# Head sums on rounded halves, and the second chunk's solve on the opposite half: a hybrid layer on one core

## The reference, cut to what matters

```python
kk = hs(k * k_k)
kk = kk / jnp.maximum(jnp.sqrt(jnp.sum(kk * kk, axis=-1, keepdims=True)), 1e-12)
...
def step(S, inp):
    r_t, w_t, k_t, v_t, kk_t, a_t = inp
    sa = jnp.einsum('bhij,bhj->bhi', S, -kk_t)
    S = (S * w_t[:, :, None, :] + sa[..., None] * (kk_t * a_t)[:, :, None, :]
         + v_t[..., None] * k_t[:, :, None, :])
    return S, jnp.einsum('bhij,bhj->bhi', S, r_t)
...
mean = jnp.mean(o, axis=-1, keepdims=True)
var = jnp.mean(jnp.square(o - mean), axis=-1, keepdims=True)
...
bonus = jnp.sum(rh * kh * r_k, axis=-1, keepdims=True) * vh
```

## Time and profile before

| | |
|---|---|
| median of 3 runs | 3245.78 us (3243.72 to 3246.97) |
| the profiled execution | 3246.72 us |
| its span, first to last instruction | 3244.7 us |
| TensorE busy | 3171.4 us (98%) |
| DVE busy | 1625.4 us (50%) |
| ACT busy | 1022.0 us (31%) |
| POOL busy | 232.5 us (7%) |
| mean granted clock of TensorE | 0.997 |

### The profile page before, as it was taken

How to read it: one execution, slowest core, us unless ns; L and a number is a source line. 1 busy time by engine, 2 the same in 40 slices (tenths; PEclk the granted TensorE clock), 3 DMA queues, 4 the chain that set the end, 5 groups by cost and what they waited for, 6 DMA issues and landing times.

```text
span 3244.7 us, 65733 instructions
## 1 busy us (share of the span) xinstructions
PE 3171.4 (98%) x27835; PEld 2663.8 (82%) x27835; DVE 1625.4 (50%) x2742; ACT 1022.0 (31%) x1858; POOL 232.5 (7%) x229
## 2 busy tenths in 40 slices
PE   8999999999999999999999999999999999999998
PEld 6777778877777878877777878998777789999997
DVE  6566554567766573454553256304555525432224
ACT  5444333344443443232222034302333312310001
POOL 0021100011011000111110000001111100000000
PEclk9999999999999999999999999999999999999999
DMA  4454443376666753554444673265343445465556
GB/s 160 155 190 161 147 154 97 104 233 203 196 215 215 254 188 97 163 157 144 138 143 146 193 237 102 92 210 167 125 124 125 134 158 168 147 192 181 176 176 196
DMA packets 269442, 532.27 MB, mean 164 GB/s; under 512 B 34016, under 2 KB 37728, under 8 KB 269152
## 3 DMA queue, kind: packets, MB, share of 16 engines
q1 hardware_dynamic: 269152, 528.07, 50.6%
HBM read 415.97 MB, written 112.08 MB: 163 GB/s over the span
## 4 chain that ended last, share of the span: by engine, by line
PE 89%; DVE 6%; DMA 2%; ACT 1%; issue 1%; SPq 0%; POOL 0%; DVEq 0%; ACTq 0%; POOLq 0%
PE PS L824 76%; PE PS L863 6%; PE PS L921 1%; PE PS L976 1%; DMA y<-xres 1%; DMA wl<-weight_lo 1%; DMA raw<-w 1%; DVE wl L1585 1%; PE PS L997 1%; PE PS L1147 1%; DVE op L2077 1%; PE PS L911 0%; PE PS L1161 0%; PE PS L1165 0%; ACT L1176 0%
## 5 line engine op out<-in xcount | busy, mean ns | idle before, releaser
L824 PE MATMUL PS<-hh,wh 128*128 128x512 f32 x1864 | 766.2, 411 | 0.9 <-ACT gst L1235 0.9
L824 PE MATMUL PS<-hh,wl 128*128 128x512 f32 x1864 | 728.9, 391 | 0.0
L824 PE MATMUL PS<-hl,wh 128*128 128x512 f32 x1864 | 727.9, 391 | 0.0
L1195 ACT ACTIVATE wh<-raw 128x512 fp32r<-128x512 f32 x452 | 284.1, 630 | 481.2 <-PE PS L824 365.7
L824 PEld LDWEIGHTS PS<-hh,wh 128*128 128x128 f32 x1864 | 350.3, 188 | 91.2 <-issue 14.3
L1585 DVE TENSOR_TENSOR wl<-raw,wh 128x512 fp32r<-128x512 f32 x452 | 321.6, 714 | 194.4 <-ACT wh L1195 189.2
L824 PEld LDWEIGHTS PS<-hh,wl 128*128 128x128 f32 x1864 | 350.4, 188 | 76.0
L824 PEld LDWEIGHTS PS<-hl,wh 128*128 128x128 f32 x1864 | 351.1, 188 | 73.7 <-issue 8.1
L824 PE MATMUL PS<-hh_last,wh 128*128 128x272 f32 x1280 | 266.1, 289 | 2.0 <-DVE xres L1717 2.0
L824 PE MATMUL PS<-hl_last,wh 128*128 128x272 f32 x1280 | 264.6, 288 | 0.0
L824 PE MATMUL PS<-hh_last,wl 128*128 128x272 f32 x1280 | 263.2, 287 | 0.0
(11 more groups left out here) (284 smaller groups left out, 4815.7 us busy)
## 6 DMA issues: line engine op xcount, KB each, us to landing
wh<-weight_hi SPq DMA_DIRECT2D x500, 256.0 KB, 2.7
wl<-weight_lo SPq DMA_DIRECT2D x500, 256.0 KB, 3.0
raw<-w SPq DMA_DIRECT2D x186, 512.0 KB, 3.6
weight_hi<-wh SPq DMA_DIRECT2D x164, 256.0 KB, 4.4
weight_lo<-wl SPq DMA_DIRECT2D x164, 256.0 KB, 4.7
raw<-w SPq DMA_DIRECT2D x76, 256.0 KB, 3.4
gate_scratch<-gst SPq DMA_DIRECT2D x48, 256.0 KB, 3.8
gb<-gate_scratch SPq DMA_DIRECT2D x24, 512.0 KB, 5.1
```

What stands on the lines that cost most here:

```text
L824: mm = pe.matmul(PS[:, bank(t) + f, 0:t.cols], wt[:, cols], mov[:, m, (t.half + f) * t.cols:(t.half + f + 1) * t.cols], start=(first and a ...
L1195: act.activation(wh[h % 4][:], src, ACT.Copy).then_inc(hi_done, 1)
```

## The change

The four head sums take two matmuls each, on a rounded part and a remainder of what is summed, against `head`, a copy of the ones matrix in fp32r that ACT makes once at the start. The rounded parts are written by ACT (`ksh`, `bh`, `mh`, `vh`), the remainders by DVE (`ksl`, `bl`, `ml`, `vl`), and the square `osq` moves from ACT to DVE as `sq`. The second chunk's solve goes from the half where it was to the opposite one: `home to own` becomes `own to home` and the reverse, S1 goes home to own and is interleaved over both chunks, and `pt1`, `yo` and `x` of the second chunk change halves on the way, which puts them on DVE in two half-tile operations each.

```diff
@@ steps @@
-        s += ["n1", "zp"] + ["lwm"] * sample + ["scan", ...]
+        s += ["ksl", "n1", "zp"] + ["lwm"] * sample + ["scan", ...]
...
-        s += ["at", "rt", "pc", "btE", "btO", "ktE", "ktO", "atl", "bv"]
-        s += each("lmE", "lmO", "ydE", "ydO") + each("xd", "svE", "svO")
+        s += ["at", "rt", "pc", "btE", "btO", "ktE", "ktO", "atl", "bl", "bv"]
+        s += each("lmE", "lmO", "ydE", "ydO") + ["pt1E1", "pt1O1"] * (not sample) + each("xd", "svE", "svO")
+        s += ["yoE1", "yoO1"] * (not sample)
@@ TensorE @@
+            def head_sum(bank_, n, hi, lo):
+                pe.matmul(PS[:, bank_, 0:n], head[:], hi[:].rearrange("p a w -> p (a w)")[:, 0:n], start=True, stop=False)
+                return pe.matmul(PS[:, bank_, 0:n], head[:], lo[:].rearrange("p a w -> p (a w)")[:, 0:n], start=False, stop=True)
...
                 yield pr.t("BO")
-                pe.wait_ge(G, pr.at("G", "bo2"))
+                pe.wait_ge(V, pr.at("V", "bl"))
                 step("bo")
-                pe.matmul(PS[:, 3, 0:4 * W], mat[:, M_HEAD], flat(cc), start=True, stop=True).then_inc(Tn, 1)
+                head_sum(3, 4 * W, pph, ccl).then_inc(Tn, 1)
...
                 yield pr.t("S1")
                 for c in pr.chs:
                     pe.wait_ge(V, pr.at("V", f"xd{c}"))
                     pe.wait_ge(A, pr.at("A", f"tok{c}"))
-                    for j in range(4):
-                        tiles(c, home, home, 5 + 2 * c, 0, of(yd[c]), of(xd[c]), j)
-                    for j in range(4):
-                        mm = tiles(c, home, home, 5 + 2 * c, 256, of(xd[c]), of(yd[c]), j)
+                for j in range(4):
+                    for c in pr.chs:
+                        tiles(c, home, own, 5 + 2 * c, 0, of(yd[c]), of(xd[c]), j)
+                for j in range(4):
+                    for c in pr.chs:
+                        mm = tiles(c, home, own, 5 + 2 * c, 256, of(xd[c]), of(yd[c]), j)
...
                 yield pr.t("MEAN")
-                pe.wait_ge(V2, pr.at("V2", f"oO{pr.chs[-1]}"))
+                pe.wait_ge(V2, pr.at("V2", "ml"))
...
                 yield pr.t("VAR")
-                pe.wait_ge(A2, pr.at("A2", "osq"))
+                pe.wait_ge(V2, pr.at("V2", "vl"))
@@ ScalarE @@
+                act.wait_ge(A, pr.at("A", "ksq"))
+                go("ksh", v4(cch), v4(pp), ACT.Copy)
...
+                yield pr.t("PTR", 0.8)
+                act.wait_ge(G, pr.at("G", "bo2"))
+                act.wait_ge(V, pr.at("V", "pc"))
+                go("bh", v4(pph), v4(cc), ACT.Copy)
...
+                yield pr.t(f"DO{pr.chs[-1]}", 0.6)
+                act.wait_ge(V2, pr.at("V2", f"oO{pr.chs[-1]}"))
+                go("mh", fl(oph), fl(oo), ACT.Copy)
                 yield pr.t("MEAN", 0.6)
                 act.wait_ge(V2, pr.at("V2", "oc"))
-                go("osq", fl(oo), fl(op), ACT.Square)
+                go("vh", fl(yol), fl(op), ACT.Square)
@@ VectorE @@
+                yield pr.t("ZA", 0.2)
+                dve.wait_ge(A, pr.at("A", "ksh"))
+                if pr.before:
+                    dve.wait_ge(G, pr.before.at("G", "lb"))
+                tt_("ksl", fl_(ktl), fl_(pp), fl_(cch), ALU.subtract)
...
+                yield pr.t("PV", 0.9)
+                dve.wait_ge(A, pr.at("A", "bh"))
+                tt_("bl", fl_(ccl), fl_(cc), fl_(pph), ALU.subtract)
                 yield pr.t("BO", 0.4)
                 dve.wait_ge(Tn, pr.at("T", "bo"))
...
+                    if c:
+                        own("ydO1")
+                        for par, name in enumerate(("E", "O")):
+                            r = home(1, par)
+                            tt_(f"pt1{name}1", pts[1][0][half_rows(par)], yd[1][r], mrep(M_XD, 4, r.start, r.stop, 64, 128), ALU.add)
...
-                    tt_(f"x{c}", yo[c][:], zl[c][:], q8(b1_), ALU.add)
+                    if c == 0:
+                        tt_("x0", yo[0][:], zl[0][:], q8(b1_), ALU.add)
+                    for par, name in enumerate(("xE1", "xO1")) if c else ():
+                        r = home(1, par)
+                        tt_(name, yo[1][r], zl[1][half_rows(par)], q8(b1_, r), ALU.add)
...
+                dve.wait_ge(A2, pr.at("A2", "mh"))
+                tt_("ml", fl_(yol), fl_(oo), fl_(oph), ALU.subtract)
                 yield pr.t("MEAN", 0.25)
...
+                own("oc")
+                tt_("sq", fl_(oo), fl_(op), fl_(op), ALU.mult)
+                dve.wait_ge(A2, pr.at("A2", "vh"))
+                own("sq")
+                tt_("vl", fl_(ool), fl_(oo), fl_(yol), ALU.subtract)
```

More of the change, by code:

```diff
@@ L249, in steps @@
     if engine == "V2":
-        s = ["x0", "saE0", "saO0"] + (["st10", "st20", "oE0", "oO0", "x1", "saE1", "saO1"] if not sample else [])
+        s = ["x0", "saE0", "saO0"] + (["st10", "st20", "oE0", "oO0", "xE1", "xO1", "saE1", "saO1"] if not sample else [])
         c = chs[-1]
-        return s + [f"oE{c}", f"oO{c}", f"st1{c}", f"st2{c}", "oc", "on", "lg", "ob", "gate"]
+        return s + [f"oE{c}", f"oO{c}", f"st1{c}", f"st2{c}", "ml", "oc", "sq", "vl", "on", "lg", "ob", "gate"]
     if engine == "A":
-        s = ["ksq", "vt", "z0", "z1", "z2", "z3", "a0", "a1", "a2", "a3", "ex", "es", "n2", "n3", "pm", "p", "ip"]
-        return s + by("ptr") + ["ath"] + by("tok", "xy2", "xy4", "x8", "d", "zl", "g", "h") + ["gc"]
+        s = ["ksq", "vt", "ksh", "z0", "z1", "z2", "z3", "a0", "a1", "a2", "a3", "ex", "es", "n2", "n3", "pm", "p", "ip"]
+        return s + by("ptr") + ["bh", "ath"] + by("tok", "xy2", "xy4", "x8", "d", "zl", "g", "h") + ["gc"]
     if engine == "A2":
-        return each("o1") + ["osq", "v1", "v2", "rwh"]
+        return each("o1") + ["mh", "vh", "v1", "v2", "rwh"]
     if engine == "G":
-        return ["kk", "cm", "kkn", "bo1", "bo2"] + by("pt1") + each("yoE", "yoO") + ["lb"]
+        return ["kk", "cm", "kkn", "bo1", "bo2", "pt10", "yoE0", "yoO0", "lb"]
     if engine == "G2":
@@ L441, in hybrid_layer @@
         hw0, ha0, hka = (new(n, [128, 4]) for n in ("hw0", "ha0", "hka"))
-        mat = new("mat", [128, M_MEAN, 128])
+        mat = new("mat", [128, M_HEAD, 128])
+        head = new("head", [128, 128], F32R)
         lora = new("lora", [128, 2, 512])
@@ L935, in front @@
                 yield pr.t("KG")
-                pe.wait_ge(V, pr.at("V", f"sub{pr.chs[-1]}"))
+                pe.wait_ge(V, pr.at("V", "ksl"))
+                if pr.first:
+                    pe.wait_ge(head_in, 1)
                 step("kn")
-                pe.matmul(PS[:, 4, 0:4 * W], mat[:, M_HEAD], flat(pp), start=True, stop=True).then_inc(Tn, 1)
+                head_sum(4, 4 * W, cch, ktl).then_inc(Tn, 1)
                 yield pr.t("PTR")
@@ L1047, in front @@
                     for c in pr.chs:
[L1048 removed]
+                        mm = tiles(c, own, home, 4 + 2 * c, 0, of(xd[c]), of(pts[c][2]), j)
                         if j == 3:
@@ L1130, in tail @@
                     for j in range(4):
-                        first = tiles(c, own, own, b1_, 0, lambda r, j, par: ra[r, j * n + c, 1, :], of(st), j)
-                        mm = tiles(c, own, other, b0_, 0, of(st), lambda r, j, par: ra[r, j * n + c, 0, :], j)
+                        first = tiles(c, own, home, b1_, 0, lambda r, j, par: ra[r, j * n + c, 1, :], of(st), j)
+                        mm = tiles(c, own, away, b0_, 0, of(st), lambda r, j, par: ra[r, j * n + c, 0, :], j)
                     step(f"q0{c}")
@@ L1547, in front @@
                 yield pr.t("XT", 0.05)
[L1548 to L1558, removed]
+                own("bo2")
+                pool.wait_ge(V, pr.at("V", "ydO0"))
+                tt_("pt10", pts[0][0][:], yd[0][:], mrep(M_XD, 4, c0=64, c1=128), ALU.add)
+                own("pt10")
+                for par, name in enumerate(("yoE0", "yoO0")):
+                    r = home(0, par)
+                    tt_(name, yo[0][r], lm[0][r, par, :, CH:128], mrep(M_YD, 4, r.start, r.stop, 64, 128), ALU.mult)
+                    own(name)
                 pool.wait_ge(V, pr.at("V", "bv"))
```

74 lines of the change are left out of this document (43 added, 31 removed).

## The result

The changed kernel takes **3309.9 us** (median of 4 runs, 3304.9 to 3312.5), the kernel before 3244.8 us beside it: ratio **1.0199**, 95% interval 1.0183 to 1.0215, 65 us slower. The forecast was 3284 us, range 3258 to 3304: right in direction, 26 us too low, and the time lies above the range. The profiled execution took 3307.4 us (span 3305.5), 60.7 us above that of before.

The account below looks back on a forecast made before the run. TensorE, busy 98% of the span, was taken as the bound. The terms summed to +38.8 us on the profiled 3246.7 us, giving 3285.5 us profiled and 3284 us as a median; range 3258 to 3304 us.

Parts of the forecast that it names:

- Sums: Head sums on TensorE: two rounded products take 0.46 us instead of 0.85 for one f32 sum; -25.6 us.
- S1: Solve stage S1 on four array quarters, interleaved over both chunks: 1.09 instead of 2.00 us a double pair; -14.6 us.
- Rival D: S1 doesn't gain because half its weight loads are exposed: +37 instead of -14.6 us, 3336 us; chance 0.04.
- BO: TensorE's sum at BO waits for `bl`, queued on DVE behind `atl`; +50 us over seventeen pairs.
- LM: TensorE's waits before LM go, since DVE catches up while TensorE stands; -2.9 us.
- VAR: The sum at VAR is released 0.75 us later by `sq`, `vh`, `vl`; only the first two pairs feel it; +1.4 us.
- MEAN: The sum at MEAN is released 1.65 us later, behind `ml`, partly hidden by spare time; +14 us.
- `x1` in halves: Two half-tile operations on DVE add 0.42 us ahead of `ds1`, where TensorE waited 7 times; +2.9 us.
- The clock: After 8 of the new stalls TensorE runs at 1.2 GHz for 3.42 us, costing 1.7 us each; +13.6 us.
- A: TensorE's clock holds, since the new stalls are single and products follow each; 3271 us; chance 0.22.
- B: DVE is no longer behind at BO, so its 50 us and the clock's 13.6 fall away; 3222 us; chance 0.09.
- C: More waits than counted, as DVE blocks on `mh` and `vh`: one more us a pair, 3301 us; chance 0.20.

Follow-up runs that it names:

- e1: The changed kernel with `bl` moved on DVE ahead of `ktE`, the tail's operations, `ktO` and `atl`; 3235.9 us.
- e9: e6 with S1's tile products issued chunk after chunk again, the second chunk still in the opposite half; 3238.8 us.
- e5: The changed kernel with unread matmuls filling TensorE's wait at BO; 3288.5 us.
- e6: e1 with MEAN's sum back on f32 operands, `mh` and `ml` left out; 3226.1 us.
- e11: The same kernel as e6, measured again on another chip; 3226.9 us.
- e3: The changed kernel with all four head sums back on f32 operands, keeping the mirrored solve with S1 on four quarters; 3238.4 us.
- e4: The changed kernel with BO's sum alone back on f32 operands, `bh` and `bl` left out; 3239.9 us.
- e2: The changed kernel with unread matmuls filling TensorE's waits at BO and, sixteen of 128 columns, at MEAN; 3300.3 us.

## Why the prediction was right in kind and wrong in size

In the order of its steps, against the profiled execution (+60.7 us measured, +38.8 forecast):

- **Sums, -25.6.** Right in the records where nothing waits: the rounded sum of e1's second pair takes 0.46 us. As time three of the four gave 4.0, 4.0 and 5.5 us for 6.4 each.
- **S1, -14.6.** 14.7 from end to end in the trace. In e9 12.0 us more from end to end cost 12.0 us of time. Rival D is out. The rule that it rested on (the Trainium skill, TensorE: Matmul & The Clock Gate, The mechanism) is contradicted a second time: in the new order every second neighbour shares a row group, and S1 took 1.10 us in the second pair; in e9's order none within a chunk does, and it took 1.84.
- **BO, +50.** The chain was right, place and order, and so was the claim that it moves along with TensorE: from PV's last product to `atl` the seventeen pairs took 103.0 us before and 104.8 after. The stalls were 52.9 us, and 15 starts from a standstill, 0.33 us longer than in a stream (a sum's 1.18 against 0.85), make it 57.9, with the start counted as the prediction's sum counts it (in the change's pairs at full clock a rounded sum ended 0.79 us after its release, against 0.46 in a stream). 5.5 of the excess are `bl` itself, stretched by `rwl`: the 0.65 us taken from back-to-back rows held only while GpSimd was still. The Trainium skill has this (SBUF - State Buffer, SBUF: two separate sides): an operation of DVE with two inputs in SBUF and one of GpSimd that reads SBUF exclude each other. The traces agree: `bl` (both inputs in SBUF) ended 0.54 us after `rwl` in nine of the ten pairs, while `atl`, with one input in PSUM, ran its 0.69 us beside it.
- **LM, -2.9; VAR, +1.4; MEAN, +14.** The wait before LM went; VAR's is 0.7 us in two pairs, 1.4 with the starts; MEAN's grew by 13.6 us, 16.6 with the starts of nine more waits.
- **`x1` in halves, +2.9.** About half of it. The wait before `ds` is 8.5 us, before it was 8.4, but that total hides a shift: in six of the seven pairs it grew, by up to 0.43 us, and in the seventh it shrank by 1.6, where the wait before SA just ahead of it, for `x1` itself, grew by 1.0. The waits before SA went from 1.0 to 2.2 us, so both together grew by 1.3. Not foreseen was that the wait for `xres` grew from 3.2 to 5.0 us.
- **The clock, +13.6: the step that failed.** I took 8 more low stretches, at most one for each of 13 candidate stalls; there were 20 more, 78.5 us at the low clock against 10.2, at the 3.42 us of the earlier trace rows for one. The 13 stalls were there, all at BO, and ten of them brought 14 stretches, four of them two each. Of the waits that I had not taken as candidates, the one of 2.11 us at BO brought one and those at MEAN two (the 2.62 us shown above and one of 2.44). The last three are the net of the waits elsewhere. The loss is 35.6 against 5.1 us, **+30.5**; what is left of the 60.7 us when all other terms are taken off is 25. e5 measured 21.4 us for BO's share alone. So the clock cost about twice the forecast, near the bound of 29 that I had set at one stretch a pair.

With the measured sizes the sum is -25.6 - 14.7 + 57.9 - 2.9 + 16.6 + 1.4 + 1.3 + 1.8 + 30.5 = +66.3, against 60.7; the loss takes every microsecond at the low clock in which TensorE worked at half, and overstates it, as e5 did. Of the 22 us by which the trace missed the forecast, 11 to 17 are the clock and 8 BO; MEAN and `xres` add 4, and `x1` takes off 2.

The rivals: A (the clock holds) and B (DVE no longer behind) are refuted by the trace. C (more waits, 3301 us) came nearest in size, mostly for the wrong cause: DVE did stand 4.7 us for `vh`, in four pairs, and 0.8 us for `mh`, but TensorE's wait at VAR is only 0.7 us. What made BO longer was that a neighbour stretched DVE's last operation.

What stays open is why one wait is followed by the low clock and another not. e6 and e11 are the same kernel with the same 3.41 us wait before the first pair's PTR:

```profile
146.82:150.24 3.42, 3.00 (x15) 2.16 (x13) 3.31 (x6) 0.60 (x2) 1.60 (x1) 1.00 1.01 389
```
```profile
147.09:150.50 3.41, 3.41 (x10) 2.74 (x9) 3.31 (x6) 1.38 (x3) 1.39 (x1) 0.50 0.78 298
```

The first window is e6's, from the first product behind the wait and PTR's transposes, at 2.4 GHz; the second e11's, from the same product, at 1.2. The two ran on different chips, but e5, on e6's chip and with the same wait of 3.41 us, fell to 1.2 there as well. The traces of e6 and e11 differ by 5.4 us in loss, the traced executions by 2.9 us and the medians by 0.8. So the count of stretches in one trace is partly a draw, and the excess loss of e3 may be one too. The medians of e1, e4 and e5 don't hang on it: their differences are far larger.

## What to carry over

When an operand of the bound engine gets one more step on another engine, look up that step's place in the other engine's queue, not its length: here 0.7 us of DVE work, put behind a chain of six operations, cost some 75 us with the clock's share, and ahead of that chain nothing. Put such a step where its own input is ready. And price a stall of TensorE at its length plus what the clock takes behind it: here the 13 stalls of 2.5 us or more at BO were followed by 14 stretches at half clock, at about 1.7 us each, and of the 14 other waits at BO and MEAN three were followed by one each. The page's clock line shows none of this.

## What the hardware showed beyond expectation

- The same 3.41 us wait of TensorE left the clock at 2.4 GHz in one execution (e6) and at 1.2 in others (e11, e5). Waits of 1.99 and 2.11 us were followed by 1.2 GHz too.
- A DVE subtraction with both inputs in SBUF, started while GpSimd's `rwl` ran, ended 0.54 us after it in both cases shown: 1.19 and 1.80 us instead of 0.69.
- In a stream, matmuls of 128 columns on rounded operands came every 0.11 us (e2), about half of the 0.23 us that 512 columns take.
